# Token-halves at the end of the out projection and of the last projection, other orders in three norm chains, gate rows by transposes, and stores issued by ScalarE too

## What is computed

```python
x = x + gate_m * rms_norm(merged @ w_out, g_post_mix)              # out projection
h2 = rms_norm(x, g_pre_ffn) * (1 + scale_f) + shift_f
f = (silu(h2 @ w_ffn_gate) * (h2 @ w_ffn_up)) @ w_ffn_down         # down projection
x = x + gate_f * rms_norm(f, g_post_ffn)
# second block
x = x + pooling_layer(rmsnorm(x, norm_a))
x = x + (attention * silu(gate)) @ w_out_b                          # last projection
return rmsnorm(x, norm_f)
```

## Time and profile before

| what | us |
|---|---|
| median of 3 runs (2493.92 to 2494.89) | 2493.96 |
| the profiled execution's own time | 2495.42 |
| its span, first to last instruction | 2493.7 |
| TensorE busy | 2430.3 |
| VectorE busy | 1613.1 |
| ScalarE busy | 1128.3 |

### The profile page before, as it was taken

How to read it: one execution, slowest core, us unless ns; L and a number is a source line. 1 busy time by engine, 2 the same in 40 slices (tenths; PEclk the granted TensorE clock), 3 DMA queues, 4 the chain that set the end, 5 groups by cost and what they waited for, 6 DMA issues and landing times.

```text
span 2493.7 us, 32659 instructions
## 1 busy us (share of the span) xinstructions
PE 2430.3 (97%) x11348; PEld 2026.1 (81%) x11348; DVE 1613.1 (65%) x2013; ACT 1128.3 (45%) x1440; POOL 1.9 (0%) x7
## 2 busy tenths in 40 slices
PE   4999999999979999999999999999999999999998
PEld 4887778888868878888888878887788899999886
DVE  7897889899766664444444454445554577777554
ACT  4544546543454343444443444444644444454443
POOL 0000000000000000000000000000000000000000
PEclk8999999999989999999999999999999999999999
DMA  9985569999848775555555556565455555545554
GB/s 373 340 321 183 159 220 354 328 331 339 294 137 272 262 263 183 182 185 177 178 189 189 185 181 200 179 202 195 160 186 194 169 156 155 161 154 172 172 183 135
DMA packets 152588, 535.98 MB, mean 215 GB/s; under 512 B 17200, under 2 KB 18480, under 8 KB 152240
## 3 DMA queue, kind: packets, MB, share of 16 engines
q1 hardware_dynamic: 150480, 527.24, 62.6%
q10 hardware_dynamic: 2016, 7.47, 0.8%
HBM read 532.55 MB, written 2.10 MB: 214 GB/s over the span
## 4 chain that ended last, share of the span: by engine, by line
PE 95%; DVE 2%; issue 1%; ACT 0%; DMA 0%; DVEq 0%; ACTq 0%; SPq 0%
PE acc L1590 29%; PE acc L1591 29%; PE acc L1592 29%; PE tb L1672 2%; PE tb L2044 1%; DVE macc L1087 1%; PE tb L1590 1%; PE tb L1591 1%; PE tb L1592 1%; PE tb L2047 0%; PE tb L2034 0%; PE tb L1795 0%; DMA start_raw<-in_wa_dram 0%; PE tb L1722 0%; DVE lo L915 0%
## 5 line engine op out<-in xcount | busy, mean ns | idle before, releaser
L915 DVE TENSOR_TENSOR lo<-raw,hi 128x1024 fp32r<-128x1024 f32 (+3 forms) x844 | 980.9, 1171 | 685.6 <-ACT hi L475 683.3
L475 ACT ACTIVATE hi<-raw 128x1024 fp32r<-128x1024 f32 (+3 forms) x844 | 851.1, 1018 | 931.4 <-PE acc L1592 791.2
L1590 PE MATMUL acc<-hi,Hh 128*128 128x512 f32 x1984 | 796.3, 401 | 1.6 <-DVE Hl L1045 1.2
L1592 PE MATMUL acc<-hi,Hl 128*128 128x512 f32 x1984 | 785.4, 396 | 0.0
L1591 PE MATMUL acc<-lo,Hh 128*128 128x512 f32 x1984 | 785.4, 396 | 0.0
L1590 PEld LDWEIGHTS acc<-hi,Hh 128*128 128x128 f32 x1984 | 373.6, 188 | 90.2 <-issue 2.8
L1592 PEld LDWEIGHTS acc<-hi,Hl 128*128 128x128 f32 x1984 | 373.2, 188 | 90.1
L1591 PEld LDWEIGHTS acc<-lo,Hh 128*128 128x128 f32 x1984 | 373.6, 188 | 87.5 <-issue 1.4
L1590 PE MATMUL acc<-hi,hbh 128*128 128x384 f32 (+1 forms) x640 | 228.3, 357 | 0.0
L1592 PE MATMUL acc<-hi,hbl 128*128 128x384 f32 (+1 forms) x640 | 222.8, 348 | 0.0
L1591 PE MATMUL acc<-lo,hbh 128*128 128x384 f32 (+1 forms) x640 | 222.7, 348 | 0.0
(11 more groups left out here) (283 smaller groups left out, 1905.7 us busy)
## 6 DMA issues: line engine op xcount, KB each, us to landing
raw<-in_wa_dram SPq DMA_DIRECT2D x680, 512.0 KB, 4.3
late_raw<-in_wa_dram SPq DMA_DIRECT2D x96, 512.0 KB, 5.2
raw<-in_wb_dram SPq DMA_DIRECT2D x128, 384.0 KB, 3.4
start_raw<-in_wa_dram SPq DMA_DIRECT2D x64, 512.0 KB, 6.2
raw<-in_wc_dram SPq DMA_DIRECT2D x64, 512.0 KB, 3.4
x<-in_x_dram ACTq DMA_DIRECT2D x2, 2048.0 KB, 9.1
out_dram<-x SPq DMA_DIRECT2D x8, 256.0 KB, 2.8
poolM<-in_pool_dram ACTq DMA_DIRECT2D x1, 768.0 KB, 6.4
```

The source lines that it names most:

```text
L475: act.activation(hi[:, s, 0:n], raw[:, r, 0:n], ACT.Copy).then_inc(hi_ready, 1)
L915: dve.tensor_tensor(lo[:, s, 0:n], raw[:, r, 0:n], hi[:, s, 0:n].bitcast(F32), ALU.subtract)\
L1590: pe.matmul(dst(tt), a, hi[:, s, w], start=first and i == 0, stop=False)
L1592: mm = pe.matmul(dst(tt), b, hi[:, s, w], start=False, stop=last and i == kts - 1)
```

## The change

- **Out projection's end.** Its fourth tile is made by `tile_by_halves`, as the down projection's. Each half has its own chain: square (ScalarE), product with gm1 and four adds of 512 columns (VectorE), four squares of x (ScalarE), sum, root and reciprocal into a second vector rstd2. VectorE scales the chunks 0 and 1 of x, ScalarE the chunks 2 and 3 (later, between splits). The square-root table is loaded in the first tile (`load_root`).
- **Between out projection and FFN.** 27 `keep_warm` matmuls, then the first pair's two tiles into banks 0 and 1, pairs 1 and 2, 3 more `keep_warm`; pairs 3 to 7 are transposed behind the units 0 to 4 of the first FFN tile, and VectorE and ScalarE split one unit between two pairs.
- **Down projection's end.** The reciprocal and the first two adds come ahead of the product of the fourth tile; 9 `keep_warm` in place of 8; the first pair goes into two banks, taken tile by tile.
- **Gate rows.** The broadcast column is transposed in place of being multiplied with the identity.
- **The end.** The gain of the last norm is loaded as a row broadcast to all partitions (nf, by ScalarE's queue, behind the last attention scores); x times the gain (xg) is made for the first three tiles as they end; the fourth is made by halves; in each half VectorE makes columns 1536 to 2047 and 1024 to 1535, which SyncE stores, ScalarE makes columns 0 to 1023 and stores them itself. The spread of the last gain is gone.

```diff
@@ scalar, out projection
-            for t in range(4):
+            for t in range(3):
                 split_to(OUT0 + 8 * t + 11)
                 square_tile(t % 2, t)
+                if t == 0:
+                    load_root()
...
-            root()
+            split_to(FFN0)
+            def square_out(tt):
+                act.activation(junk[:, tt, :], acc[:, 2 + tt, :], ACT.Square, accum_out=ssqp[:, tt, 3:4]).then_inc(half_squared, 1)
+                c.up("squared")
+                half_root(tt, base + 1)
+            def square_sum(tt):
+                for i in range(4):
+                    act.wait_ge(x2_ready, c.up("x2"))
+                    act.activation(junk_x[:, tt, chunk(i)], x[:, tt, chunk(i)], ACT.Square, accum_out=ssqp[:, tt, i:i + 1])\
+                        .then_inc(half_squared, 1)
+                    c.up("squared")
+            act.wait_ge(half_done, c.up("half"))
+            square_out(0)
             split(1)
-            square_x()
-            root()
+            square_sum(0)
+            finished(FFN0 - 1)
+            square_out(1)
+            half_root(0, base + 2)
+            split(1)
+            square_sum(1)
+            half_root(1, base + 3)
+            split(1)
...
+            act.wait_ge(tr_split, c.up("split"))
+            scaled_hi(0, 0, 0).then_inc(first_hi, 1)
+            act.wait_ge(tr_split, c.up("split"))
+            act.wait_ge(first_scaled, 1)
+            scaled_hi(1, 1, 0).then_inc(tr_hi, 1)
+            for k in (1, 2):
+                take_scaled(k)
+            act.wait_ge(half_rstd, c.up("rstd", 2 * TT))
+            scale_x(2)
+            split(1)
+            take_scaled(3)
+            split(1)
+            scale_x(3)
+            for k in range(4, KD // 2):
+                take_scaled(k)
+                split(1)
@@ vector, out projection
+            def add_out(tt):
+                dve.wait_ge(half_squared, c.up("squared"))
+                dve.tensor_tensor(mix[:, tt, 3 * N:], acc[:, 2 + tt, :], gm1[:, 3 * N:], ALU.mult).then_inc(acc_free[2 + tt], 1)
+                half_inverse(rstd, tt)
+                dve.wait_ge(acc_free[2 + tt], TILES_BEFORE_OUT // 2 + 3)
+                for i in range(4):
+                    dve.scalar_tensor_tensor(x[:, tt, chunk(i)], mix[:, tt, chunk(i)], rstd[:, tt:tt + 1], x[:, tt, chunk(i)],
+                                             ALU.mult, ALU.add).then_inc(x2_ready, 1)
+            def scale_x(tt):
+                half_inverse(rstd2, tt)
+                for i in range(2):
+                    dve.tensor_scalar(mix[:, tt, chunk(i)], x[:, tt, chunk(i)], rstd2[:, tt:tt + 1], None, ALU.mult)\
+                        .then_inc(xn_ready, 1)
-            add_normed(mix)
+            add_out(0)
             split(1)
...
+            sum_x(0)
+            add_out(1)
+            scale_x(0)
+            sum_x(1)
+            scale_x(1)
...
+            dve.wait_ge(tr_split, TURNED_BEFORE_FFN + 2)
+            scaled(1, 1, 0, 0).then_inc(first_scaled, 1)
+            dve.wait_ge(first_hi, 1)
+            chain(scaled(0, 0, 0, 0))
+            dve.wait_ge(tr_hi, c.up("hi"))
+            split_x(0).then_inc(tb_free[0], 1)
+            dve.sem_inc(tb_free[1], 1)
+            split(1)
@@ tensor, out projection
+            tile_by_halves(mergedh, mergedl, 1, 8)
+            read_out(0)
+            keep_warm(0, 27, mergedh, mergedl)
...
+            turn_x(1)
+            turn_x(2)
+            keep_warm(0, 3, mergedh, mergedl)
...
-            tile(Hh, Hl, 0, 8, before=when_split(split_by))
+            tile(Hh, Hl, 0, 8, before={k: (lambda k=k: pe.wait_ge(*split_by[k])) for k in range(KD // 2)},
+                 after={k: (lambda k=k: turn_x(k + 3)) for k in range(KD // 2 - 3)})
@@ vector, down projection
             for tt in range(TT):
-                dve.wait_ge(half_squared, c.up("squared"))
+                half_inverse(rstd, tt)
+                for i in range(2):
+                    add_chunk(tt, i)
                 dve.tensor_tensor(fmix[:, tt, 3 * N:], acc[:, 2 + tt, :], gm2[:, 3 * N:], ALU.mult).then_inc(acc_free[2 + tt], 1)
-                half_inverse(rstd, tt)
...
-            take_pair(0)
+            for kt in range(2):
+                dve.wait_ge(first_normed, kt + 1)
+                dve.scalar_tensor_tensor(Hl[:, kt, :], tb[:, kt, 0:T], vec("norm_a", kt), Hh[:, kt, :].bitcast(F32),
+                                         ALU.mult, ALU.subtract).then_inc(tb_free[kt], 1)
@@ tensor, gate rows (spread_gate_m; spread has the same edit)
-                    ins = pe.matmul(tb[:, 2, j * P:(j + 1) * P], fG[:, 4 * q + j:4 * q + j + 1].to_broadcast([P, P]), ident[:],
-                                    start=True, stop=True)
+                    ins = pe.transpose(tb[:, 2, j * P:(j + 1) * P], fG[:, 4 * q + j:4 * q + j + 1].to_broadcast([P, P]), ident[:])
@@ scalar, the end
+            for tt in range(TT):
+                act.wait_ge(acc_free[2 + tt], n + 1)
+                act.activation(junk[:, tt, :], x[:, tt, 3 * N:], ACT.Square, accum_out=ssqp[:, tt, 3:4]).then_inc(half_squared, 1)
+                c.up("squared")
+                half_root(tt, base)
+                act.wait_ge(half_rstd, c.up("rstd"))
+                for q in range(2):
+                    act.activation(x[:, tt, q * N:(q + 1) * N], xg[:, tt, q * N:(q + 1) * N], ACT.Copy, scale=rstd[:, tt:tt + 1])\
+                        .then_inc(out_scaled, 1)
+                act.wait_ge(out_scaled, 2 * (tt + 1))
+                act.dma_start(out[tt * P:(tt + 1) * P, 0:2 * N], x[:, tt, 0:2 * N]).then_inc(stored, 16)
@@ vector, the end
-                    dve.scalar_tensor_tensor(xt, xt, rstd[:, tt:tt + 1], tb[:, q, :], ALU.mult, ALU.mult).then_inc(out_ready, 1)
+                dve.tensor_tensor(x[:, tt, n], acc[:, 2 + tt, :], x[:, tt, n], ALU.add).then_inc(acc_free[2 + tt], 1)
+                half_inverse(rstd, tt)
+                dve.scalar_tensor_tensor(x[:, tt, n], x[:, tt, n], rstd[:, tt:tt + 1], nf[:, n], ALU.mult, ALU.mult)\
+                    .then_inc(out_ready, 1)
+                dve.tensor_scalar(x[:, tt, 2 * N:3 * N], xg[:, tt, 2 * N:3 * N], rstd[:, tt:tt + 1], None, ALU.mult)\
+                    .then_inc(out_ready, 1)
```

More of the change, by code:

```diff
@@ L437, in _ @@
             stream(wc, 0, C_UNITS)
[L438 to L442, removed]
+            for tt in range(TT):
+                for i, q in enumerate((3, 2)):
+                    sp.wait_ge(out_ready, 2 * tt + i + 1)
+                    sp.dma_start(out[tt * P:(tt + 1) * P, q * N:(q + 1) * N], x[:, tt, q * N:(q + 1) * N]).then_inc(stored, 16)
+            sp.wait_ge(stored, 3 * TT * 16)
         @block.gpsimd
@@ L734, in _, with scale_x @@
                 ins.then_inc(tr_hi, 1)
-            def hidden(n):
-                split(8)
+            def scale_x(i):
+                for tt in range(TT):
+                    ins = act.activation(mix[:, tt, chunk(i)], x[:, tt, chunk(i)], ACT.Copy, scale=rstd2[:, tt:tt + 1])
+                ins.then_inc(xs_ready, 1)
+            assert c.n["split"] == TURNED_BEFORE_FFN
+            act.wait_ge(tr_split, c.up("split"))
+            scaled_hi(0, 0, 0).then_inc(first_hi, 1)
+            act.wait_ge(tr_split, c.up("split"))
@@ L738, in hidden @@
+            act.wait_ge(first_scaled, 1)
[11 more added lines that the diff above has]
+                split(1)
+            def hidden(n, first=8):
+                split(first)
                 tile_done()
@@ L741, in hidden @@
                 take_hi_tile(hidh, n * 4)
-            for n in range(FFN_MOD):
+            hidden(0, FFN0 + 12 - c.n["unit"])
+            for n in range(1, FFN_MOD):
                 hidden(n)
@@ L887, in _ @@
                 ins.then_inc(evac, 1)
-            root()
+                if i == 0:
+                    load_root()
+            split(4)
+            n = c.up("acc1")
+            base = c.up("base")
+            for tt in range(TT):
+                act.wait_ge(acc_free[2 + tt], n + 1)
[8 more added lines that the diff above has]
+                act.dma_start(out[tt * P:(tt + 1) * P, 0:2 * N], x[:, tt, 0:2 * N]).then_inc(stored, 16)
         @block.vector
@@ L1374, in _ @@
+            base_of(slice(0, TT))
             dve.wait_ge(x_loaded, 2 * 16)
-            add_normed(mix)
-            split(1)
[L1377 to L1384, removed]
+            c.up("half")
@@ L1385, in _ @@
+            dve.wait_ge(tr_split, TURNED_BEFORE_FFN + 2)
[6 more added lines that the diff above has]
+            split(1)
+            for k in range(1, KD // 2):
                 dve.wait_ge(tr_hi, c.up("hi"))
                 for j in range(2):
[L1387 removed]
@@ L1395, in hidden @@
-            def hidden(n):
-                split(16)
+                split_x(k).then_inc(tb_free[(k + 1) % 4], 1)
+                split(1)
+            def hidden(n, units=16):
+                split(units)
                 tile_done()
@@ L1401, in hidden @@
```

(3 more changed lines are left out.)

148 lines of the change are left out of this document (99 added, 49 removed).

## The result

| | before | after |
|---|---|---|
| median, us | 2494.02 (4 runs, 2493.92 to 2494.89) | 2429.40 (4 runs, 2427.13 to 2430.10) |
| the profiled execution, time and span | 2495.42, 2493.7 | 2430.10, 2428.3 |

The ratio is 0.9739, 95% interval 0.9722 to 0.9755: 64.6 us less. The forecast was 2473.8 (2471.0 to 2478.0): the sign was right, the amount was off by 44.4 us, and the range did not hold it.

The account below looks back on a forecast made before the run. TensorE, busy 2430.3 of 2493.7 us, bounds the kernel, leaving its idle holes, low clock and own work; 11.8 + 0.6 + 2.9 + 4.9 = 20.2 us off gives 2473.8 us at the median, range 2471.0 to 2478.0.

Parts of the forecast that it names:

- Part 1: Out projection's end up to the FFN: half-by-half chain, keep-warm matmuls and transposes between units shorten the gap; gain 11.8 us.
- The 9.55: First FFN matmul 9.55 us after E, which is the issue of the out projection's last matmul plus 0.233.
- rival (a): Clock falls in the new hole behind the out projection: matmuls cost 2.4 us, transposes 1, giving 2477; chance 0.10.
- Part 2: Down projection's end: adds start sooner, so the second block's first matmul comes earlier; gain 0.6 us, bounds 0 and 0.9.
- Part 3: Gate rows as transposes at half the price: 1.8 us in the out stage, 1.1 before down; together 2.9.
- rival (d): Gate rows: transposes of a broadcast cost what the matmuls did, giving 2476.7; chance 0.05.
- Part 4: Program's end: gain 4.9 us; bounds 6.4 (big store lands after 2.8 us) and 2.8 (after 6.4 us).
- (b): First eight FFN units: VectorE or ScalarE sets the pace, TensorE waits 4.2 us, giving 2478; chance 0.10.
- (c): Program's end: ScalarE's store lands late, after 6.4 us, giving 2475.9; chance 0.12.
- (e): FFN: the clock doesn't come back, slower than before, 2511 if it lasted through two tiles; chance 0.03.

Follow-up runs that it names:

- e2: The changed kernel with 32 bytes left free ahead of Hh, putting Hh and all behind it back on their addresses of before; 2475.83 us.
- f4: The changed kernel without the 27 and the 3 keep-warm matmuls between out projection and FFN; 2431.21 us.
- g4: The kernel before with one 32-byte tile (mv) allocated ahead of hi instead of behind fm, so hi and lo move by 32 bytes and Hh doesn't; 2446.42 us.
- f1: The kernel before with 96 bytes left free ahead of Hh (offset 128); 2490.49 us.
- f2: The changed kernel with 128 bytes left free ahead of Hh (offset 128); 2473.21 us.

## Why the prediction was wrong, and what of it was right
**The step that failed** stands in the prediction's opening, on what bounds the kernel: "so 12 matmuls are 2.80 us and one is 0.233 us". It is right of the kernel before, and the sum then took it for the kernel after as well. Nothing in the prediction asks where the tiles lie, though its own diff takes 64 bytes from fm and adds a tile of 32. There is no term, no bound and no rival for a matmul that takes another time after the change. It was worth 46.4 us (2475.83 to 2429.40 on the changed kernel) and 47.9 (2494.28 to 2446.42 on the kernel before), more than twice the 20.2 of all that was costed.

**Part 1**, forecast 11.8. On e2, at the old spacing: 26.46 - 13.07 - 4 x 0.43 for the transposes still to come = 11.7; the table of starts gives 13.19 - 1.57 = 11.6. The 9.55 was 9.83 in fact: on the changed kernel's own trace the adds start at E + 1.72 as forecast (682.41), the transposes at E + 6.91 against 6.8, and the rest lies in the hand-overs of the first pair. The clock never fell, and rival (a), once its condition was made, cost 2.3 us (f4), a third less than its price of 3.4.

**Part 2**, forecast 0.6: 15.05 - 14.33 = 0.72. **Part 3**, forecast 1.8 and 1.1: 1.57 + 0.29 = 1.86 and 14.33 - 13.19 = 1.14; a broadcast column transposes at the price of any other (four rows with a wait in 2.41 us, where the products took 3.55), so rival (d) is out. **Part 4**, forecast 4.9: 19.7 - 15.05 = 4.7; the large store took 3.9 us from its issue to its landing, between the bounds 2.8 and 6.4. Rivals (b), (c) and (e) did not come: the clock is at 1.00, units are 3.21 us apart behind the first (693.70, 696.91, 700.11), and no store is late.

The four measure 20.0 us together. The spans differ by 19.7, since e2 was 0.29 behind at 607 us; the medians by 18.5 (2494.30, the kernel before timed beside it, to 2475.83), since the profiled execution of before lay 1.4 above its median and e2's (2475.80) on its own. On the good placement the change is worth 17.0 us by the medians (2446.42 to 2429.40), 1.5 less, which is no more than the runs scatter. But the starts show a loss of that size in one place: the changed kernel leads g4 by 12.08 us at 733 and by 10.24 at 918 (732.90 against 744.99, 917.56 against 927.79), in the stretch in which the changed kernel's execution has its two waits, 2.3 us, and g4's has none.

It is the same for the placement. The starts of the changed kernel against e2 run apart by 2.8% where TensorE sets the pace (from 15.14 us at 918 to 29.17 at 1413), not at all between 1960 and 2260 (41.38 to 41.14), where the matmuls have 384 columns or fewer, and by 1.7% from 733 to 918 (12.08 to 15.14). The kernel before and g4, whose chains have no load there, run apart by 4.98 us over the same instructions (187.78 us against 182.80), that is 2.7%. These 1.9 us are about what lies between the 46.4 of the one pair and the 47.9 of the other. Most of the rest up to the 53 of the count is missing ahead of 598 us: some 2,050 matmuls times 0.0066 are 13.5 us there, and the starts are 9.0 apart (606.86 and 597.83). These runs don't say what takes the rest in that part.

## What to carry to other kernels
Ahead of costing an edit's instructions, look at what it does to the allocation: here sixteen columns less in a small tile moved every tile behind it. A multiple of 256 bytes between all stationary and moving operands was worth 2.8% of each matmul of 512 columns, and one tile out of line gave most of it away in the stages that read it. An experiment that changes two things, code and layout, is best run a second time with a pad that puts the tiles back: only that told what the change itself was worth.

## What was not expected of the hardware
- The spacing of 512-column matmuls depends on where the stationary tiles begin relative to the moving ones, at equal clock and equal instructions: 0.2267 us at 0 and 256 bytes, 0.2333 at 32, 64 and 224, 0.2325 at 128, 0.2343 at 96. At 2.4 GHz that is 544 cycles against 560 for 512 columns. Both ends moved together change nothing (2428.83 us).
- It is not a sum of pairs: with Hl and the tiles behind it off, the two products with Hh show the long 400 and 399 ns, and the longest step from start to start is the one ahead of the product with Hl. Hh 32 and Hl 64 off (0.2312) was better than either all at 32 or all at 64. This stays open.
- Matmuls of 384 columns show 335 to 336 ns with starts 0.174 us apart at both 0 and 32 bytes; at 128 (f1 and f2) their starts are 0.176 apart.
- The clock's fall behind the out projection, avoided by 30 matmuls without a use, cost 2.3 us where it happened and 1.8 at the end of the program by the medians, within their spread; in the two profiled executions nothing of it is left at the end (spans 2428.1 and 2428.3).
